# Where the gate weights' low half is computed: GpSimd instead of VectorE in the expert stage

## What is computed

```python
xb = xf[row_tok].reshape(n_blocks, MOE_BLOCK, -1)

def expert_block(args):
    xblk, e = args
    return (jax.nn.silu(xblk @ w_gate[e]) * (xblk @ w_up[e])) @ w_down[e]

yb = lax.map(expert_block, (xb, blk_e)).reshape(rows, -1).astype(F32) * row_w[:, None]
return jnp.zeros(xf.shape, F32).at[row_tok].add(yb).astype(xf.dtype)
```

## Time and profile before

| what | value |
|---|---|
| median of three runs | 3528.32 us |
| the profiled execution, its own time | 3537.32 us |
| its span, first to last instruction | 3535.4 us |
| TensorE matmul, weight load: busy | 3054.5 us (86%), 2644.6 us (75%) |
| VectorE, ScalarE, GpSimd: busy | 1779.2 us (50%), 1468.4 us (42%), 453.6 us (13%) |
| granted TensorE clock, mean | 0.929 |
| weight load of the expert stage, one piece | 2048 KB, gate lands after 12.9 us (median) |

### The profile page before, as it was taken

How to read it: one execution, slowest core, us unless ns; L and a number is a source line. 1 busy time by engine, 2 the same in 40 slices (tenths; PEclk the granted TensorE clock), 3 DMA queues, 4 the chain that set the end, 5 groups by cost and what they waited for, 6 DMA issues and landing times. The chain is left out here.

```text
span 3535.4 us, 62407 instructions
## 1 busy us (share of the span) xinstructions
PE 3054.5 (86%) x22878; PEld 2644.6 (75%) x22879; DVE 1779.2 (50%) x2685; ACT 1468.4 (42%) x2924; POOL 453.6 (13%) x430
## 2 busy tenths in 40 slices
PE   7999999989996899945749997799339999999998
PEld 7999999978885788833527885588228787777876
DVE  5244065545554455543316773344436766676562
ACT  5112155345554555520212331355135655555452
POOL 1000000000000000010400000111232222222222
PEclk9999999989998899976869998899569999999999
DMA  5333433133344211123933333433158988988792
GB/s 165 115 118 134 144 123 116 69 108 115 127 145 119 68 50 62 44 76 97 290 105 125 128 130 107 157 132 138 38 197 292 334 264 280 309 293 300 226 314 60
DMA packets 299074, 549.16 MB, mean 155 GB/s; under 512 B 80133, under 2 KB 136083, under 8 KB 298350
## 3 DMA queue, kind: packets, MB, share of 16 engines
q1 hardware_dynamic: 259790, 406.64, 34.2%
q0 software_dynamic: 34864, 137.67, 12.3%
q10 hardware_dynamic: 4224, 2.10, 0.2%
HBM read 436.53 MB, written 143.43 MB: 164 GB/s over the span
## 5 line engine op out<-in xcount | busy, mean ns | idle before, releaser
L136 PE MATMUL pj_pu<-pj_w,pj_nT 128*128 128x256 f32 (+3 forms) x1088 | 307.0, 282 | 0.0
L137 PE MATMUL pj_pu<-pj_w,pj_nT 128*128 128x256 f32 (+3 forms) x1088 | 306.1, 281 | 0.0
L138 PE MATMUL pj_pu<-pj_w,pj_nT 128*128 128x256 f32 (+3 forms) x1088 | 305.5, 281 | 0.0
L3135 ACT ACTIVATE ex_gate<-ex_gate_raw 128x2048 fp32r<-128x2048 f32 x64 | 119.1, 1908 | 239.3 <-DMA ex_gate_raw<-in_w_gate 164.1
L137 PEld LDWEIGHTS pj_pu<-pj_w,pj_nT 128*128 128x128 f32 (+1 forms) x1088 | 202.3, 186 | 0.0
L138 PEld LDWEIGHTS pj_pu<-pj_w,pj_nT 128*128 128x128 f32 (+1 forms) x1088 | 202.2, 186 | 0.0
L136 PEld LDWEIGHTS pj_pu<-pj_w,pj_nT 128*128 128x128 f32 (+1 forms) x1088 | 201.9, 186 | 0.1
L3198 DVE TENSOR_TENSOR ex_gate<-ex_gate_raw,ex_gate 128x2048 fp32r<-128x2048 f32 x64 | 143.7, 2287 | 101.9 <-ACT ex_gate L3135 101.9
L716 ACT ACTIVATE att_prob<-att_score,att_res 128x256 f32<-128x256 f32 (+1 forms) x384 | 127.6, 444 | 142.6 <-DVE att_res L752 142.6
L3198 DVE TENSOR_TENSOR ex_down<-ex_down_raw,ex_down 128x2048 fp32r<-128x2048 f32 x64 | 143.8, 2288 | 74.6 <-ACT ex_down L3135 74.6
L136 PE MATMUL pj_pu<-pj_nT,pj_w 128*128 128x384 f32 (+2 forms) x480 | 175.4, 365 | 0.0
(11 more groups left out here) (568 smaller groups left out, 7943.4 us busy)
## 6 DMA issues: line engine op xcount, KB each, us to landing
ex_gate_raw<-in_w_gate SPq DMA_DIRECT2D x32, 2048.0 KB, 12.9
ex_up_raw<-in_w_up SPq DMA_DIRECT2D x32, 2048.0 KB
ex_down_raw<-in_w_down SPq DMA_DIRECT2D x32, 2048.0 KB
out_win_k<-in_cache_k POOLq DMA_DIRECT2D x8, 2032.0 KB, 13.0
out_win_v<-in_cache_v POOLq DMA_DIRECT2D x8, 2032.0 KB, 13.6
tmp_att<-att_res POOLq DMA_DIRECT2D x48, 264.0 KB, 4.5
pout_att<-tmp_att SPq DMA_DIRECT2D x16, 792.0 KB, 4.5
pj_raw<-in_w_in SPq DMA_DIRECT2D x24, 512.0 KB
```

The source lines that it names most:

```text
L136: pe.matmul(out, ah, bh, start=start, stop=False)
L137: pe.matmul(out, ah, bl, start=False, stop=False)
L138: return pe.matmul(out, al, bh, start=False, stop=stop)
L3135: act.activation(half[p][:, 0, part(p, h)], raw[p][:, part(p, h)], ACT.Copy).then_inc(E[p + "_hi"], 1)
```

## The change

GpSimd gets `lower_gate`: if an expert begins in block b+2, it waits for each high half of the gate weights and subtracts it from the raw weights, two instructions of 128x2048. It stands in GpSimd's turn for block b behind the load of the list of indices and ahead of the scatter. VectorE loses the same two instructions and the reading of the flag at the end of its turn. Gates of blocks 0 and 1, split ahead of the loop, stay on VectorE (L3209, L3213 before), so 30 of 32 move. ScalarE, SyncE and TensorE keep their code.

```diff
+                def lower_gate(b):
+                    with pool.If(read(pool, 2, b, 1)):
+                        r = began(pool, b)
+                        for h in range(2):
+                            pool.wait_ge(E["g_hi"], 2 * r + h)
+                            pool.sem_inc(E["seen"], 1)
+                            pool.tensor_tensor(half["g"][:, 1, part("g", h)], raw["g"][:, part("g", h)], half["g"][:, 0, part("g", h)].bitcast(F32),
+                                               ALU.subtract).then_inc(E["g_split"], 1)
+
                 def work(i, u, b, q):
                     v = 1 - u
                     pool.wait_ge(E["x_turned"], b + 2)
...
                     load_rows(v, b + 5)
+                    lower_gate(b + 2)
                     pool.wait_ge(E["y_ok"], 2 * b + 4)
                     pool.wait_ge(E["added"], 16 * b + 16)
...
                     lower_if("u", b + 1)
                     rows(u, b + 2)
-                    lower_if("g", b + 2)
```

## The result

The changed kernel takes 3701.03 us (median of four runs, 3698.76 to 3702.62); the kernel before took 3530.68 beside it. The ratio is 1.0481, 95% interval 1.0465 to 1.0498: slower by 170 us, where 57 were forecast. The sign and the place were right, the size was three times too small and the time lies above the range.

The account below looks back on a forecast made before the run. TensorE was taken to bound the alternating blocks and the transfers to pace the runs. Queue 43 plus collisions 14 gave 57 us, on 3528.3 a forecast of 3585 us; range 3542 to 3640.

Parts of the forecast that it names:

- GpSimd's price: GpSimd's moved subtractions: 4.55 us each for 2048 columns, interpolated between two rows; about 10.0 us an expert with flag and waits.
- The slack it consumes: GpSimd's waits for output rows: 292.6 us of slack, against 300 us for 30 experts, making it as loaded as TensorE.
- VectorE's relief: VectorE's loop: losing 60 instructions, 137 us, gives back little more than the first wait of each run.
- The queue, 43 us: Runs of expert blocks: GpSimd's longer rounds, 23 to 24.5 us where blocks took 20, lose 43 us in all.
- The walk: Expert stage: GpSimd's rounds followed block by block from scatter to list load, plus 10.0 us an expert, giving 43 us.
- just fit: Alternating blocks: GpSimd needs about 34.5 us of a pair's 35.4, so it costs nothing there.
- the alternating pairs tip too: Rival, alternating blocks: 1 or 2 us more in every round overdraws their 0.9 us slack; 3620 to 3658 us, chance 0.20.
- run side by side: Gate load to ready, 15 us, beside GpSimd's own 14.7: at most some tenths a block, none added.
- The same inside a run is covered by GpSimd's round: Collisions of VectorE's and GpSimd's subtractions: counted only at the ends of six runs, since GpSimd's round covers those inside.
- The range: Whole kernel: 3542 to 3640 us, leaving out the near tie, the faster case and the upper end of the tipped pairs.
- 43 + 41: Top of the forecast case, 3625 us: queue loss 43 plus the collisions' upper end 41, and some tenths a block.
- the forecast's own 14: Collisions of VectorE and GpSimd at the shared on-chip memory: 2.3 us for each of six runs, 14 us.

Follow-up runs that it names:

- psum_second: The changed kernel, but VectorE's up and down subtractions read their second operand from a spare PSUM bank of zeros: 3622.98 us, ratio 1.0274.
- psum_two_raw: The changed kernel with a second raw gate buffer and the second operand of VectorE's subtractions in PSUM: 3567.46 us, ratio 1.0105.

## Why the prediction was wrong in size

- **GpSimd's price: right.** 4545 ns by interpolation, 4575 undisturbed. An expert costs 1.0 + 9.1 + 0.2 = 10.3 us; 10.0 was said.
- **The slack it consumes: right.** The wait for output rows went to 27.4 us (under 60 was said), TensorE waits up to 4.6 us for GpSimd and up to 6.4 for VectorE at a time, and no gain was hidden in VectorE's relief.
- **The queue, 43 us: the first step that failed.** The walk is that of a kernel with one buffer and no collisions, and `psum_second`, which is that kernel, loses 94. The lengths inside a run were right: behind its first block a block takes 24.1 to 24.6 us (23.1 to 24.6 in the walk), and from the gate load to the pair it is 2764.93 - 2749.79 = 15.1 us (15 in the prediction).

Two other things were wrong. The walk lets GpSimd enter the run with the lead that it had in the kernel before: the scatter of block 5 was to leave 6.7 us ahead of P of block 6 and left 3.7 ahead of it (2749.79, P at 2753.52), and the first block of the run took 24.7 us (to P of block 7 at 2778.26) where the walk has 20.2. And the alternating pair, which with 34.5 us of 35.4 was to "just fit", does not fit after a run: its two gathers wait 8.44 and 9.73 us, where the rows that it was added up from have 5.54 and 9.53. The two P and GpSimd's pair, from the timelines of `psum_second`:

```profile
2753.52 0.39 PE L136 MATMUL ex_py<-ex_down,ex_hT 128*128 128x512 f32 x1
...
2778.26 0.39 PE L136 MATMUL ex_py<-ex_down,ex_hT 128*128 128x512 f32 x1
```
```profile
2863.26 1.64 POOL L3127 DMA_INDIRECT out_y<-ex_y,ex_place  x1 [1.36 <-issue]
...
2875.25 0.56 POOL L3080 DMA_DIRECT2D ex_idx<-tmp_i_rows  x1 [8.44 <-DMA ex_xb<-tmp_hn,ex_idx]
...
2899.42 0.56 POOL L3080 DMA_DIRECT2D ex_idx<-tmp_i_rows  x1 [9.73 <-DMA ex_xb<-tmp_hn,ex_idx]
2901.25 1.63 POOL L3127 DMA_INDIRECT out_y<-ex_y,ex_place  x1 [1.27 <-issue]
```

That is 38.0 us from scatter to scatter. By its blocks `psum_second` loses 72 us in the runs and 20 between them, where the walk has 42 and 1. So part of the rival "the alternating pairs tip too" came true; in the changed kernel the blocks between the runs lose 25.6 us. The prediction let the gate load and GpSimd's round "run side by side" and added nothing. They are not independent: with a second buffer, which lets the load leave earlier, the loss falls from 94 to 38, so 56 us hang on the one buffer. That the load does this through the gathers is read from their waits and was not tried.

- **That `psum_two_raw` loses 38, close to the 43, is luck.** It has a second buffer, which the walk has not, and 28 of the 43 us between its first and last P are in the runs and 15 between them.
- **"The same inside a run is covered by GpSimd's round": the second step that failed,** 76 us where 14 stood and the upper bound was 41. Where GpSimd is the bound, its round has no cover to give. In the round shown GpSimd's pair loses 2.0 us and the scatter's issue 1.9, and VectorE's product comes 6 us late. The rows for the second of these were there: the scatter of 2.75 us among those of 1.65. So the two engines had met in the expert stage as well, and not only in the delta net stage.
- **The range** took its top from 43 + 41 and the tipped pairs. With 94 in place of the 43 the forecast's own 14 would have given 3528 + 108 = 3636, and the 76 for the collisions takes it past 3640.

## What to carry to other kernels

Moving work to an idle engine costs what that engine's queue waits for, not what its busy share says: walk one whole round, with its transfers, and then every loop that passes through the moved instruction, above all one with a single buffer in it. Begin the walk a few rounds early, without the lead that the engine had before the change. Where two engines shut each other out, as VectorE and GpSimd do here, they can meet in round after round once one of them is the bound, so price a collision per round and ask who is queued behind both. And first ask what the relief is worth: here a kernel in which the moved work was nearly free gained nothing.

## What the runs showed of the chip that was not expected

VectorE's subtraction with both operands in SBUF can hold up the issue of an indirect transfer on GpSimd: 3.50 us beside it, 1.64 without, and the mean over 48 scatters fell from 2548 to 1642 ns when VectorE's operand came from PSUM. The kernel before shows it too, in VectorE's and GpSimd's timelines beside the scatter of 2.75 us:

```profile
2764.97 4.48 DVE L3198 TENSOR_TENSOR ex_down<-ex_down_raw,ex_down 128x2048 fp32r<-128x2048 f32 x2
```
```profile
2765.98 1.18 POOL L3082 DMA_DIRECT2D ex_place<-tmp_i_rows  x1
2767.46 2.89 POOL L3088 DMA_INDIRECT ex_xb<-tmp_hn,ex_idx  x1 [0.30 <-issue]
```

The gather, an indirect transfer, took 2.89 to issue beside the subtractions, for 1.01 without; the plain load of places ran beside them as well and stayed at 1.2. One operand from PSUM ended the contention at no price to VectorE itself, 2284 ns for 2288.
